# A hybrid attention / DeltaNet / expert-retrieval step: the last two token tiles gather joined U and V rows of 8 KB instead of separate rows of 4 KB

## What is computed

```python
q = (hf @ w_pq).reshape(T, 8, 2, 128)
s = einsum('thpd,hpnd->thpn', q, sub_keys)
sv, si = top_k(s, 16)
cand = sv[:, :, 0, :, None] + sv[:, :, 1, None, :]       # 256 candidates per head
cidx = si[:, :, 0, :, None] * 128 + si[:, :, 1, None, :]
top_s, pos = top_k(cand, 16)
eidx = take_along_axis(cidx, pos)                        # 128 experts per token, of 16384
gates = softmax(top_s)
act = einsum('td,nd->tn', hf, expert_u)
coef = gates * gelu(take_along_axis(act, eidx))
dense = zeros(T, 16384).at[tokens, eidx].add(coef)
out = dense @ expert_v
```

## Time and profile before

| | |
|---|---|
| median of 3 runs | 1422.61 us |
| lowest and highest run | 1419.26, 1423.8 us |
| span of the profiled execution | 1577.7 us |
| mean granted TensorE clock in it | 0.770 |
| VectorE busy | 813.6 us, 52% |
| TensorE matmuls busy | 865.6 us, 55% |
| GpSimd busy | 749.9 us, 48% |
| data moved | 486.09 MB |
| of them by the queue of the gathers | 404.28 MB |

### The profile page before, as it was taken

How to read it: one execution, slowest core, us unless ns; L and a number is a source line. 1 busy time by engine, 2 the same in 40 slices (tenths; PEclk the granted TensorE clock), 3 DMA queues, 4 the chain that set the end, 5 groups by cost and what they waited for, 6 DMA issues and landing times.

```text
span 1577.7 us, 14365 instructions
## 1 busy us (share of the span) xinstructions
PE 865.6 (55%) x4990; PEld 500.8 (32%) x4990; DVE 813.6 (52%) x2047; ACT 277.6 (18%) x662; POOL 749.9 (48%) x794
## 2 busy tenths in 40 slices
PE   4999998799567776787620675400442005500254
PEld 2566867556353355543210651000110001100010
DVE  2443234687484277851597146897515760087301
ACT  4234443122241232421000020000100000000000
POOL 0001000453446644456676226676667666676663
PEclk9998999899798999899755887655685557755576
DMA  9234446995659988799999729999999999999996
GB/s 394 91 140 151 161 167 254 375 390 215 240 182 356 343 310 316 241 395 352 364 404 357 297 72 375 359 397 364 354 376 376 402 346 335 359 402 364 347 368 234
DMA packets 120295, 486.09 MB, mean 308 GB/s; under 512 B 13344, under 2 KB 14240, under 8 KB 115616
## 3 DMA queue, kind: packets, MB, share of 16 engines
q0 software_dynamic: 111056, 404.28, 68.4%
q1 hardware_dynamic: 9168, 80.90, 13.2%
HBM read 482.50 MB, written 2.62 MB: 307 GB/s over the span
## 4 chain that ended last, share of the span: by engine, by line
DVE 17%; issue 17%; PE 14%; POOL 13%; DMA 6%; another core or an unknown queue 4%; ACT 1%; POOLq 0%; DVEq 0%; ACTq 0%
PE bank L1357 13%; DVE big L2086 11%; POOL big L988 10%; DMA big<-in_ev,idx 2%; POOL big L977 2%; DMA big<-in_ev,rowT 2%; DMA big<-in_eu,consts 2%; DVE hT L2086 1%; POOL hT L988 1%; PE bank L1363 1%; PE bank L1475 0%; DVE big L1876 0%; DVE dn_tok L1970 0%; DVE sq L2112 0%
## 5 line engine op out<-in xcount | busy, mean ns | idle before, releaser
L2086 DVE CUSTOM_DVE_ANT_0 big<-big,hnow 128x1024 f32<-128x1024 f32 x315 | 377.4, 1218 | 193.2 <-DMA big<-in_eu,consts 127.9
L1357 PE MATMUL bank<-big,W 128*32 128x512 f32 x1296 | 259.7, 835 | 167.6 <-DMA big<-in_ev,idx 64.0
L977 POOL DMA_INDIRECT big<-in_eu,consts x236 | 223.4, 947 | 103.4 <-issue 71.6
L988 POOL DMA_INDIRECT big<-in_ev,rowT x197 | 190.5, 967 | 153.5 <-PE bank L1357 76.6
L1357 PE MATMUL bank<-hT,wring 128*128 128x128 f32 (+1 forms) x896 | 143.3, 319 | 40.4 <-issue 32.2
L1363 PE MATMUL bank<-consts 128*128 128x128 f32 x6 | 2.4, 392 | 294.3 <-DVE consts L2101 294.3
L1357 PEld LDWEIGHTS bank<-big,W 128*32 128x32 f32 x1296 | 53.4, 136 | 332.3 <-issue 319.7
L988 POOL DMA_INDIRECT big<-in_ev,idx x118 | 111.7, 947 | 68.2 <-issue 33.3
L1357 PEld LDWEIGHTS bank<-hT,wring 128*128 128x128 f32 x896 | 120.4, 202 | 64.6 <-issue 41.4
L1357 PE MATMUL bank<-big 128*128 128x128 f32 x720 | 100.1, 288 | 40.6 <-issue 23.0
L977 POOL DMA_INDIRECT big<-in_eu,idx x79 | 75.1, 951 | 99.1 <-DVE coef L2086 57.4
(11 more groups left out here) (294 smaller groups left out, 1379.8 us busy)
## 6 DMA issues: line engine op xcount, KB each, us to landing
wring<-in_wch SPq DMA_DIRECT2D x29, 2048.0 KB, 9.2
big<-in_wch SPq DMA_DIRECT2D x6, 1536.0 KB, 8.8
big<-in_eu,consts POOLq DMA_INDIRECT x236
big<-in_ev,rowT POOLq DMA_INDIRECT x197
tok<-in_wch SPq DMA_DIRECT2D x6, 512.0 KB, 9.9
big<-in_ev,idx POOLq DMA_INDIRECT x118
xs<-in_x SPq DMA_DIRECT2D x1, 1536.0 KB, 6.6
out_y<-xs SPq DMA_DIRECT2D x3, 512.0 KB
```

Source lines behind the costliest of these rows:

```text
L977: nc.gpsimd.indirect_dma_start(row(slot), None, eu, bass.IndirectOffsetOnAxis(ap=idx[t][:, n:n + 1], axis=0)).then_inc(rows_in[slot], 16)
L988: nc.gpsimd.indirect_dma_start(row(slot), None, ev, bass.IndirectOffsetOnAxis(ap=rowT[t][:, n:n + 1], axis=0)).then_inc(rows_in[slot], 16)
L1357: return nc.tensor.matmul(out, lhsT, rhs, start=first, stop=last)
L2086: V.tensor_tensor_reduce(row(slot), row(slot), hnow[:, :], 1.0, 0.0, ALU.mult, ALU.add, coef[t % 2][:, n:n + 1]).then_inc(dot_ready, 1)
```

## The change

For tiles 1 and 2 U and V rows are gathered together. The host lays `expert_u` and `expert_v` side by side as `euv`, rows of 8 KB. Tile 0 keeps its 256 gathers in the old form. Then come 256 gathers `gw`, one per slot of tile 1 and tile 2, each of 128 rows of 8 KB (1 MB), by the untransposed numbers. They land in joined slots: six in `big` for tile 1 (each covers two old rows) and, for tile 2, four more in `wring`. Tile 0's last 48 gathers (places 208 to 255) use slots 4 to 11 and 20, nine in place of thirteen, so that the first two joined slots lie clear of tile 0.

The U half of a joined slot is used by `dot` as before. Then, for every pair of slots, ScalarE applies gelu to two columns (`gelu`), VectorE makes two 128x128 diagonal matrices of gelu times gate (`spread`), in eight places in `W`, and TensorE multiplies each with the V half of its slot (`v_slot`): two float32 matmuls of 128x128 against 128x512, added into the same accumulators. A joined slot is free when its `v_slot` is done. The transposed numbers, the coefficient transposes and the fills are gone for tiles 1 and 2. The planner's table `EARLIER` gets higher values for tile 2's `experts` steps of the second half (400) and for the first two `last_norm` steps.

```diff
-STAGES = [..., (208, [4, 5, 6, 7, 8, 9, 10, 11, 20]), (768, [0, 1, 2, 3, 4, 5, 6, 7, 8, 9, 10, 11, 20])]
+STAGES = [..., (256, [4, 5, 6, 7, 8, 9, 10, 11, 20])]
-HALVES = [(t, a) for t in range(NT) for a in range(2)]
-ALONE = {(0, 0): 64, (0, 1): 64, (1, 0): 64, (1, 1): 64, (2, 0): 64}
+HALVES = [(0, 0), (0, 1)]
+WIDE0 = ROWS + 13
+WIDE = {1: range(WIDE0, WIDE0 + 6), 2: range(WIDE0, WIDE0 + 10)}
+SPREADS = 8
 def gather_order():
+    out = []
+    for a in range(2):
+        out += [("gu", 0, HALF * a + n) for n in range(HALF)]
+        out += [("gv", 0, a, b, j) for b in range(BATCHES) for j in range(QUADS)]
+    return out + [("gw", t, n) for t in (1, 2) for n in range(SLOTS)]
 def row_homes():
+        under = [slot]
+        if last[slot] < 0 and WIDE0 <= slot < WIDE0 + 6:
+            under = [2 * (slot - WIDE0), 2 * (slot - WIDE0) + 1]
+        out[g] = (slot, 16 * uses[slot], [GATHERS[last[u]] for u in under if last[u] >= 0])
-EARLIER = {..., ('experts', 2, 1, 1): 100.0, ...}
+EARLIER = {..., ('experts', 2, 1, 1): 400.0, ..., ('experts', 2, 1, 0): 400.0, ('last_norm', 0): 300.0, ('last_norm', 1): 150.0}
 def row(slot):
+            if slot >= WIDE0:
+                m = 2 * D * ((slot - WIDE0) % 6)
+                return (big if slot < WIDE0 + 6 else wflat)[:, m:m + 2 * D]
+        def spread_at(t, n):
+            m = (SLOTS * (t - 1) + n) % SPREADS
+            return W[m // 4][:, P * (m % 4):P * (m % 4) + P]
 def row_free(gather):
+                if slot >= WIDE0 + 6:
+                    pool.wait_ge(*product.at("pq", 3, 2))
+                elif slot >= WIDE0:
+                    pool.wait_ge(*product.at("o", *PAIRS[2][0]))
+            def wide_rows(t, n):
+                if n % QUARTER == 0:
+                    pool.wait_ge(*idx_ready.at(t, n // QUARTER))
+                slot, _ = row_slot(("gw", t, n))
+                row_free(("gw", t, n))
+                nc.gpsimd.indirect_dma_start(row(slot), None, euv,
+                                             bass.IndirectOffsetOnAxis(ap=idx[t][:, n:n + 1], axis=0)
+                                             ).then_inc(rows_in[slot], 16)
+            def gelu(t, b):
+                c = coef[t % 2][:, 2 * b:2 * b + 2]
+                act.wait_ge(dot_ready, SLOTS * t + 2 * b + 2)
+                nc.scalar.activation(c, c, ACT.Gelu).then_inc(*gelu_ready.next(t, b))
+            def v_slot(t, n):
+                if n == 0:
+                    pe.wait_ge(*acc_read.at(t - 1))
+                slot, count = row_slot(("gw", t, n))
+                pe.wait_ge(rows_in[slot], count)
+                pe.wait_ge(*spread_ready.at(t, n // 2))
+                for h in range(2):
+                    ins = mm(acc[h][:, :], spread_at(t, n), row(slot)[:, D + 512 * h:D + 512 * h + 512], n == 0, n == SLOTS - 1)
+                ins.then_inc(vsum_done, 1)
 def dot(t, n):
-                V.tensor_tensor_reduce(row(slot), row(slot), hnow[:, :], 1.0, 0.0, ALU.mult, ALU.add,
+                u = row(slot)[:, 0:D]
+                V.tensor_tensor_reduce(u, u, hnow[:, :], 1.0, 0.0, ALU.mult, ALU.add,
                                        coef[t % 2][:, n:n + 1]).then_inc(dot_ready, 1)
+            def spread(t, b):
+                old = SLOTS * (t - 1) + 2 * b + 1 - SPREADS
+                dve.wait_ge(vsum_done, 2 * BATCHES + max(old + 1, 0))
+                dve.wait_ge(*gelu_ready.at(t, b))
+                for n in (2 * b, 2 * b + 1):
+                    ins = V.scalar_tensor_tensor(out=spread_at(t, n), in0=ident, scalar=coef[t % 2][:, n:n + 1],
+                                                 in1=gates[t][:, n:n + 1].to_broadcast([P, P]), op0=ALU.mult, op1=ALU.mult)
+                ins.then_inc(*spread_ready.next(t, b))
```

More of the change, by code:

```diff
@@ L121, in row_slot @@
     return HOMES[gather][:2]
-OPS_ROWS = [g for g in GATHERS if HOMES[g][0] > ROWS + 8]
+OPS_ROWS = [g for g in GATHERS if HOMES[g][0] in range(ROWS + 9, WIDE0)]
 def row_user(gather):
-    return ("dot",) + gather[1:] if gather[0] == "gu" else ("v_batch",) + gather[1:4]
+    return {"gu": ("dot",) + gather[1:], "gv": ("v_batch",) + gather[1:4], "gw": ("v_slot",) + gather[1:]}[gather[0]]
 class Counts:
@@ L509, in expert_steps @@
         after = [("@", 1, GATHERS[n - 1])] if n else [(k,) + td for td in PAIRS[0] for k in ("dn_scores", "dn_qg")]
[L510 removed]
+        after += [("expert_rows", t, g[2])] if g[0] == "gv" else [("experts", t, g[2] // HALF, g[2] // QUARTER % 2)]
         slot, _, back = HOMES[g]
+        after += [row_user(b) for b in back]
         if back:
[L513 removed]
+            pass
+        elif slot >= WIDE0 + 6:
+            after += [("query", 3, 2)]
+        elif slot >= WIDE0:
+            after.append(("dn_done",) + PAIRS[2][0])
         elif slot > ROWS + 8:
@@ L683, in program @@
         gates = [Q[:, Q_LAM + P * i:Q_LAM + P * (i + 1)] for i in (0, 1, 0)]
-        rowT = [sb(f"rowT{i}", [P, P], i32) for i in range(2)] + [idx[0]]
+        rowT = [sb(f"rowT{i}", [P, P], i32) for i in range(2)]
         coef = [sb("coef", [P, SLOTS]), K[:, C_COS:C_COS + P]]
@@ L942, in first_states @@
                 pool.dma_start(S[:, :, :], s0).then_inc(s0_in, 16)
-            held = {"gu": 0, "gv": 0}
+            held = {"dots": 0, "sums": 0}
             def row_free(gather):
                 slot, _, back = HOMES[gather]
-                if back:
-                    done, count = used_up(back)
-                    if count > held[back[0]]:
-                        pool.wait_ge(done, count)
-                        held[back[0]] = count
+                for b in back:
+                    done, count = used_up(b)
+                    kind = "dots" if b[0] == "gu" else "sums"
+                    if count > held[kind]:
+                        pool.wait_ge(done, count)
+                        held[kind] = count
+                if back:
+                    return
+                if slot >= WIDE0 + 6:
+                    pool.wait_ge(*product.at("pq", 3, 2))
+                elif slot >= WIDE0:
+                    pool.wait_ge(*product.at("o", *PAIRS[2][0]))
                 elif slot > ROWS + 8:
```

98 lines of the change are left out of this document (49 added, 49 removed).

## The result

The changed kernel takes 1475.73 us (median of 4 runs, 1472.68 to 1491.95) against 1422.38 for the kernel before: ratio 1.040, interval 1.035 to 1.046, **slower**. The forecast was 1358 us, faster.

A forecast was written before the change was run, and what follows sets the result against it. GpSimd's issue and the DMA engines were taken to bound the kernel alike, 1.25 us per gather. For tiles 1 and 2, 731 + 8 us becomes 643 + 20 + 7 + 4 = 674, -65 from 1422.6: 1358 us, range 1305 to 1425.

The forecast's parts named there:

- mostly the profile's own: TensorE's crawl and GpSimd's 54 us gap were taken as largely absent from the runs, leaving 731 us plus 8.
- (1): Tiles 1 and 2: 256 gathers of 8 KB rows at 2.51 us each, 643 us, with GpSimd's issue no longer limiting.
- rival B: Rows of 8 KB are served slower than two of 4 KB, 2.96 us each, giving 1473 us; chance 0.04.
- (2): TensorE's sums per joined slot: 1.8 to 3.5 us, 2.25 at a guessed clock of 0.8, covered by the 2.51 us transfer.
- Rival A: TensorE stays at the half clock and bounds the joined slots at 3.5 us each, giving 1592 us; chance 0.08.
- (3): VectorE per joined slot: dot, diagonal matrix and wait for gelu, 1.8 us of 2.51.
- (4): Tile 2's choice work on VectorE, some 55 us, put ahead by `EARLIER`: 0 to 40 us exposed, 20 taken.
- (6): Tile 0's last 48 gathers on nine slots, at most 5 us, plus 2 us waiting for slot 2: together 7 us.
- (5): Six joined slots give 2.2 to 2.7 us per gather, which holds tightly for tile 1; tile 2 has ten.
- rival D: Small lookahead and choice work starve tile 1: +23 us and choice 40 instead of 20, giving 1401 us; chance 0.20.
- (7): Kernel's end: work after the last landing grows from 3.64 us to 6 to 9 us, +4.
- rival C: Static order delays tile 0 or tile 2's choice beyond the gain, or crawl hits sums; over 65 us: slower, chance 0.04.

The follow-up runs named there:

- the probe: The kernel before, unchanged, profiled on a chip where it takes about 1422 us: 1421.62 us, profiled span 1419.7 us.
- e1: The kernel before, unchanged, profiled anew on a chip where it takes about 1586 us: 1582.31 us, ratio 1.000.
- e6: The kernel before, unchanged, profiled beside a run of the changed kernel on a slower chip: 1588.9 us in a single run.
- e5: The changed kernel, unedited, on a chip where the kernel before takes 1595.48 us: 1535.13 us, ratio 0.963.
- e15: The changed kernel with each joined slot filled by two gathers of 4 KB rows, on a 1422 us chip: 1497.42 us, ratio 1.054.
- e8: The kernel before with tile 0's last 48 gathers on nine row slots, on a 1586 us chip: 1587.44 us, ratio 1.002.
- e14: The changed kernel with tiles 1 and 2's query matmuls cut to two of eight, on a 1422 us chip: 1468.37 us, ratio 1.033.
- e7: The changed kernel with tile 0's last V batch raised by one more `EARLIER` entry, on a 1586 us chip: 1584.2 us, ratio 0.999.
- e2: The changed kernel with the whole `EARLIER` table of the kernel before, on a 1586 us chip: 1520.98 us, ratio 0.961.
- e3: The changed kernel with only tile 2's `experts` entries of `EARLIER` put back, on a 1586 us chip: 1523.24 us, ratio 0.965.
- e12: The changed kernel planned with lower costs for `v_slot`, `top_key` and `dot`, without tile 2's `experts` bonuses, on a 1422 us chip: 1465.64 us, ratio 1.029.

## Why the prediction was wrong

**The baseline.** The prediction took the 54 us hole out of the profile's 785 us and said that in the runs 739 us remain for the 512 gathers. The probe has 675.3. The hole is indeed not in the runs on 1422 chips, but neither is the rest of the lost time: the four U halves of tiles 1 and 2 take 88 to 90 us instead of 80 to 88, the four V halves 90 to 99 instead of 85 to 90, 56 us in all, and some 49 us more are lost ahead of tile 1. With the 54 that is the whole difference of the two profiles, 158 us, to within 1 us, and e1 and e6 show the same on their chips. The first step that failed is "mostly the profile's own": 155 us between span and median were put down to one visible stall of 54, and the other 100 were left without a place. With 675.3 in the place of 739 the prediction's own sum would have been 1422.6 - 675.3 + 674 = 1421 us, no change. On a 1586 chip the same sum (785 becomes 674 in a profile of 1577.7) gives 1467, and e5's span is 1533.9: the sign was right there, and most of the 67 us between them is again the late start (69 us, of which 7 were in the sum).

**(1) Transfer and issue**: 2.51 us per slot taken, ends 2.42 and 2.96. Measured, 667.2 us for 256 slots to the last use; in the undisturbed stretch one pair per 4.97 us. Rows of 8 KB run at 422 GB/s where two gathers of 4 KB rows ran at 409 (e15). Right, towards the low end; rival B is out. Every stretch of joined gathers (395 to 422 GB/s) lies above the limit of about 358 GB/s that the prediction quoted from the Trainium skill ("DMA: Bandwidth & Descriptors", section Specifications). The same page, section Bandwidth, keeps that figure for two cores that stream at once and has 425 GB/s for a 16 MB transfer by one; with one core at 422, this case agrees with that part.

**(2) The sums**: 1.8 us per slot at the full clock, right. The last pairs on TensorE, and what follows the last on VectorE:

```profile
1449.00 3.67 PE L1409 MATMUL bank<-wring,W 128*128 128x512 f32 x8 [1.30 <-DVE W L2170]
1453.96 3.67 PE L1409 MATMUL bank<-big,W 128*128 128x512 f32 x8 [1.29 <-DVE W L2170]
1459.85 3.67 PE L1409 MATMUL bank<-big,W 128*128 128x512 f32 x8 [2.22 <-DVE W L2170]
```

```profile
1457.52 1.22 DVE L2146 CUSTOM_DVE_ANT_0 big<-big,hnow 128x1024 f32<-128x1024 f32 x1 [1.24 <-DMA big<-in_euv,consts]
...
1459.09 0.61 DVE L2170 SCALAR_TENSOR_TENSOR W<-consts,coef,params 128x128 f32<-128x128 f32 x2 [0.34 <-ACT coef L1361]
1463.56 0.69 DVE L2182 TENSOR_TENSOR sq<-bank,gate 128x512 f32<-128x512 f32 x1 [3.85 <-PE bank L1409]
```

Eight records in 3.67 us, then a wait of 1.3 us for the next spread. The granted clock was guessed at 0.8 and is 0.92 to 0.99 at 71 to 76% busy. Rival A is out, though every pair waits 1.3 us before it starts. The Trainium skill ("TensorE: Matmul & The Clock Gate", section HAM oscillation) tells of a kernel whose groups of matmuls each wait for a transfer and start at the low clock. Its waits are longer than the 1.3 us here, so the joined slots do not contradict it; that short waits would do the same, as the prediction feared, these slots do not show.

**(3) VectorE**: a `spread` is two instructions in 0.61 us, a gelu 0.2. Right.

**(4) Tile 2's choice** was priced at 20 us among the slots. Two of tile 2's four quarters are there, in the second stretch of 64 gathers. From issue to issue it takes 167.6 us, against 159 at the free pace of 2.485: some 9 us. (The third stretch is shorter than the free pace because four more slots let GpSimd run ahead.) The other two quarters, and all four of tile 1, lie ahead of the slots, in tile 0's stage, see (6). By the probe half of the choice that the prediction saw beside tile 1's first V half was not tile 2's but tile 1's.

**(5) Lookahead**: the DMA share is 0.98 to 1.01 in all four stretches. Right; rival D is out.

**(6) Tile 0 and the handover**: 7 us, measured 65. This is the second step that failed. Of the two things that were priced, the nine slots cost what was said (e8); the landing order was not measured alone. What the sum left out is the order of the plan. By the traces, 2 of the 16 query steps of tiles 1 and 2 stand ahead of the third V batch of tile 0's second half before the change, and 12 after it; ahead of the ninth batch 4 and then all 16. On VectorE six choice quarters of tiles 1 and 2 are done before tile 1's first dot, and two in the probe. Before, twelve query steps ran beside a U half, where TensorE has little to do by itself (5.6 of 80 us), and six choice quarters beside V halves, where VectorE has 12 us to do. The joined slot needs both engines all the time, so both fallow stages are gone, and the planner puts the work where it still fits: tile 0's V half, whose rows then wait. The prediction costed the removal of the transposes and the cover of the choice, but it had no term for the queries, which were the work of the very hole that it had in front of it. That they stand in the hole, and that GpSimd waits for the V batch behind them, the trace shows. That they alone are not the price, e14 shows: three quarters of them gone give back 12 of the 65 us. That VectorE's choice is what stands behind them fits e14's busy times and e7's third wait, but no run takes the choice away. Three other orders (e2 and e3, e7, e12) won nothing, lost 57 us, and won 10 to 16 us.

**(7) The tail**: +4, measured +3.3 from the last use.

**The rivals.** What happened is rival C's first case, at a chance of 0.04. In numbers: with the right baseline the prediction's sum is 1421, no change; 58 us of handover above the 7 make it 1479, and 1475.7 was measured. C needed "over 65 us" only because the baseline was wrong by 64; with the right one, any lateness above nothing decides against the change. Whether an order exists that starts tile 1 near 725 us and still fits the queries and the choice among the slots stays open: no version tried here beat the kernel before on a 1422 chip.

## What to carry to other kernels

Before a term is taken out of a profile as "not in the runs", every microsecond between span and median wants a place; what can't be placed belongs in the range, since it may change the baseline of every stage. When two phases with different engines are merged into one that keeps both busy, list all other work that ran in the shade of either, with its length, and ask of a written-out order where it goes; here some 50 us of TensorE and 64 of VectorE lost their shade for a gain of 17 in the transfer.

## What the runs showed that was not expected

- The same kernel takes 1422 us on some chips and 1586 to 1595 on others. On the latter TensorE issues one record per 2.1 us, or none for 63 us, with nothing shown that it waits for, and a U half of 64 gathers of 4 KB rows takes 88 to 90 us instead of 80 (88 for tile 1's first), while joined gathers of 8 KB rows keep their pace. What lies behind it stays open.
- How far a change pays depends on this: 0.963 on a 1586 chip, 1.040 on a quick one.
- Expert rows of 4 KB stream at 409 to 411 GB/s, rows of 8 KB at 422, into one core. Whether GpSimd's 1.25 us per gather or the length of the row holds the former down was not separated.
